# The last strips of a feed-forward block in another order: two up projections, then three down projections

## The reference, cut to what matters

```
h = rms_norm(x, pre_mlp_g)
m = jnp.square(jax.nn.relu(h @ w_up)) @ w_down        # w_up 2048 x 8192, w_down 8192 x 2048
x = x + rms_norm(m, post_mlp_g)
```

## Time and profile before

| | |
|---|---|
| timed executions | 1083.80, 1084.32, 1084.45 us, median 1084.32 |
| profiled execution | 1082.61 us, its span 1080.6 us |
| TensorE busy | 1064.9 us, 99% of the span |
| VectorE, ScalarE, GpSimd busy | 694.3, 513.4 and 94.1 us |
| granted TensorE clock, mean | 0.998 of full |

### The profile page before, as it was taken

How to read it: one execution, slowest core, us unless ns; L and a number is a source line. 1 busy time by engine, 2 the same in 40 slices (tenths; PEclk the granted TensorE clock), 3 DMA queues, 4 the chain that set the end, 5 groups by cost and what they waited for, 6 DMA issues and landing times.

```text
span 1080.6 us, 13612 instructions
## 1 busy us (share of the span) xinstructions
PE 1064.9 (99%) x4874; PEld 885.6 (82%) x4874; DVE 694.3 (64%) x766; ACT 513.4 (48%) x655; POOL 94.1 (9%) x102
## 2 busy tenths in 40 slices
PE   9999999999999999999999999999999999999996
PEld 7888888888888788888888888888888888888875
DVE  6465565558975677575665765756657656566586
ACT  6564445445544564444444444444444444444443
POOL 0010120120000420000000000000000000000003
PEclk9999999999999999999999999999999999999999
DMA  9765455453755555666656766666576665675642
GB/s 336 277 217 181 155 167 174 146 192 131 298 195 195 156 178 183 219 201 203 214 167 230 216 201 207 190 214 214 174 234 210 204 207 171 215 234 173 237 156 78
DMA packets 114655, 214.73 MB, mean 199 GB/s; under 512 B 7232, under 2 KB 20160, under 8 KB 113856
## 3 DMA queue, kind: packets, MB, share of 16 engines
q1 hardware_dynamic: 114480, 214.27, 61.0%
q10 hardware_dynamic: 144, 0.04, 0.0%
HBM read 204.84 MB, written 2.10 MB: 192 GB/s over the span
## 4 chain that ended last, share of the span: by engine, by line
PE 93%; DVE 3%; ACT 1%; issue 1%; POOL 1%; DMA 0%; SPq 0%; DVEq 0%; POOLq 0%; ACTq 0%
PE ps L635 30%; PE ps L637 30%; PE ps L636 30%; PE ps L643 2%; DVE w_lo L1182 1%; DVE aT_raw L1223 1%; DMA raw<-in_w_in 0%; PE ps L817 0%; DVE acc L1242 0%; PE ps L871 0%; PE ps L822 0%; DVE xT_lo L1408 0%; ACT u_sb L1004 0%; POOL x_res L1629 0%; ACT w_hi L917 0%
## 5 line engine op out<-in xcount | busy, mean ns | idle before, releaser
L1182 DVE TENSOR_TENSOR w_lo<-raw,w_hi 128x1024 fp32r<-128x1024 f32 (+2 forms) x383 | 470.0, 1235 | 333.9 <-ACT w_hi L917 331.4
L917 ACT ACTIVATE w_hi<-raw 128x1024 fp32r<-128x1024 f32 (+2 forms) x383 | 397.2, 1039 | 468.9 <-PE ps L637 461.3
L635 PE MATMUL ps<-w_hi,xT_hi 128*128 128x512 f32 (+1 forms) x800 | 313.1, 391 | 2.6 <-DVE xT_lo L1268 1.4
L637 PE MATMUL ps<-w_lo,xT_hi 128*128 128x512 f32 (+1 forms) x800 | 309.4, 387 | 0.0
L636 PE MATMUL ps<-w_hi,xT_lo 128*128 128x512 f32 (+1 forms) x800 | 309.2, 386 | 0.0
L635 PE MATMUL ps<-w_hi,yT_hi 128*128 128x512 f32 x672 | 263.1, 392 | 2.7 <-DVE yT_lo L1202 2.7
L637 PE MATMUL ps<-w_lo,yT_hi 128*128 128x512 f32 x672 | 261.7, 389 | 0.0
L636 PE MATMUL ps<-w_hi,yT_lo 128*128 128x512 f32 x672 | 261.6, 389 | 0.0
L635 PEld LDWEIGHTS ps<-w_hi,xT_hi 128*128 128x128 f32 x800 | 150.5, 188 | 35.0 <-issue 3.6
L637 PEld LDWEIGHTS ps<-w_lo,xT_hi 128*128 128x128 f32 x800 | 150.3, 188 | 30.5
L636 PEld LDWEIGHTS ps<-w_hi,xT_lo 128*128 128x128 f32 x800 | 150.5, 188 | 28.7
(11 more groups left out here) (147 smaller groups left out, 428.5 us busy)
## 6 DMA issues: line engine op xcount, KB each, us to landing
raw<-in_w_up SPq DMA_DIRECT2D x64, 1024.0 KB, 5.4
raw<-in_w_down SPq DMA_DIRECT2D x64, 1024.0 KB, 6.2
raw<-in_w_in SPq DMA_DIRECT2D x28, 1024.0 KB, 5.2
raw<-in_w_o SPq DMA_DIRECT2D x16, 1024.0 KB, 5.1
aT_raw<-a_blk SPq DMA_DIRECT2D x224, 32.0 KB, 1.9
raw<-in_w_uq SPq DMA_DIRECT2D x8, 576.0 KB, 4.0
raw<-in_w_ukv SPq DMA_DIRECT2D x4, 1024.0 KB, 5.0
raw<-in_w_in SPq DMA_DIRECT2D x7, 512.0 KB, 8.4
```

The costliest lines, as they stand in the source:

```text
L635: nc.tensor.matmul(dst, x_hi, hi, start=first, stop=False)
L637: mm = nc.tensor.matmul(dst, x_hi, lo, start=False, stop=last)
L917: nc.scalar.activation(w_hi[:, slot, 0:size], raw[:, raw_slot, first:first + size], ACT.Copy).then_inc(hi_ready, 1)
L1182: nc.vector.tensor_tensor(w_lo[:, slot, 0:size], raw[:, raw_slot, first:first + size], f32(w_hi[:, slot, 0:size]), ALU.subtract).then_inc( ...
```

## The change

The loop ends one iteration earlier. The tail is up strip 14, up strip 15, down strips 13, 14 and 15. Up strip 15 sums in banks 2 and 3 and no longer waits for the relu of the strip ahead. Both last strips are turned by `turn_blocks` and moved by 16 DMAs each; the transposed operands of strips 14 and 15 lie in slots 4 and 8 of `yT`. The sync engine issues the moves behind the loads of the tail's quads 2, 8 and 12.

```diff
-SHIFTED = (0, FF_STRIPS - 1)
+A_SLOT = {FF_STRIPS - 2: 4, FF_STRIPS - 1: 8}
...
-    n = len(quads) + 8 * (FF_STRIPS - 3) - 1
+    n = len(quads) + 8 * (FF_STRIPS - 4) - 1
+    for q in range(4):
+        products(up(j - 1, q, n := n + 1), tail)
+    tail.append(("relu", j - 1, n))
     for q in range(4):
         products(up(j, q, n := n + 1), tail)
+        if q == 0:
+            tail.append(("a_turn", j - 1, 0))
     tail.append(("relu", j, n))
     for q in range(4):
-        n = down(j - 1, q, n + 1)
-        for k in range(4):
-            tail.append(("mm", n, k))
-            if k == 1 and q in (1, 2):
-                tail.append(("a_shift", j, 2 * q - 1))
+        products(down(j - 2, q, n := n + 1), tail)
+        tail.append(("add", 4 * (j - 2) + q, n))
+        if q == 0:
+            tail += [("a_turn", j, 0), ("aT", j - 1, A_SLOT[j - 1])]
+    for q in range(4):
+        products(down(j - 1, q, n := n + 1), tail)
         tail.append(("add", 4 * (j - 1) + q, n))
-        if q < 2:
-            tail.append(("a_shift", j, 2 * q))
-        if q == 2:
-            tail.append(("aT", j, 4))
+        if q == 0:
+            tail.append(("aT", j, A_SLOT[j]))
...
-    LOOP = range(2, FF_STRIPS - 1)
+    LOOP = range(2, FF_STRIPS - 2)
...
-            return 6 if j == 1 else 0
+            return {1: 6, FF_STRIPS - 1: 2}.get(j, 0)
...
-                if n == NQ_TAIL + 2:
-
-                    sp.wait_ge(aT_lo_ready, FF_STRIPS - 2)
-                    move_blocks(FF_STRIPS - 1)
+                if n in (NQ_TAIL + 2, NQ_TAIL + 8, NQ_TAIL + 12):
+
+                    j = FF_STRIPS - {2: 3, 8: 2, 12: 1}[n - NQ_TAIL]
+                    sp.wait_ge(aT_lo_ready, j)
+                    move_blocks(j + 1)
...
-                        elif z["j"] > 1 and z["q"] == 0:
+                        elif 1 < z["j"] < FF_STRIPS - 1 and z["q"] == 0:
...
-                    at = 4 if z["j"] == FF_STRIPS - 1 else 0
+                    at = A_SLOT.get(z["j"], 0)
...
-                    hidden_hi(a, b, a in SHIFTED)
+                    hidden_hi(a, b, a == 0)
...
-                    turn_blocks(a, None)
+                    turn_blocks(a, (a - 1) * 256 if a > 1 else None)
```

More of the change, by code:

```diff
@@ L951, in hidden_hi @@
                 if shifted:
-                    act.wait_ge(a_turned, j + 1)
+                    act.wait_ge(a_turned, 1)
                 else:
```

## The result

| | before | changed |
|---|---|---|
| median of the timed executions (four each) | 1084.06 us | 1090.55 us (1090.02 to 1091.23) |
| profiled execution, span | 1080.6 us | 1088.7 us |
| granted clock, mean | 0.998 | 0.994 |

The ratio is 1.0063, with a 95% interval of 1.0051 to 1.0076: 6.5 us slower. 1091.5 was forecast, in a range of 1087.2 to 1095.5.

A forecast was written before the change was run, and what follows sets the result against it. PE, busy 1064.9 of 1080.6 us, was taken as the bound. Late quad 13 (8.65) minus old stall (2.9) plus clock (1.5) gave +7.2 us, from 1084.3 to 1091.5 us, range 1087.2 to 1095.5.

The forecast's parts named there:

- The two late loads: Tail loads of quads 9 and 13, each issued behind 16 moves: quad 9 starts 1.0 us late, quad 13 8.65 us.
- GpSimd's square: GpSimd's 1.9 us square in the tail, ending near 5.2 us after quad 9's landing, was claimed to delay nothing.
- L + 10.4: With L quad 9's landing at 1006.9, the end of strip 14's `yT_lo` at 1017.3, when the second moves can start.
- L + 20.8: With L quad 9's landing at 1006.9, the time quad 13's load is issued, behind the second group of moves.
- The Trainium skill's fit for a transfer: 2.0 us plus bytes by 436 GB/s: a load takes 4.4 us, the two late loads cost 3.8 us less; not used.
- The clock: PE's 7.2 us stall before quad 13 drops the clock to 1.2 GHz, costing 1.5 us, between nothing and 3.0.
- The rival with the clock unchanged: Loads late in the tail but the clock stays: +5.7 us, 1090.0 us; chance 0.16.
- What is taken out: Two large transposes replace strip 15's 16 small ones, so PE's 2.9 us wait before its down quads goes.
- The old stall: PE's wait in the tail of the kernel before, until 1049.48, for DVE's `yT_lo`: called 2.9 us.
- the loads are in time: Rival: the second moves do not delay quad 13 beyond the old stall, 1081.4 us; chance 0.06.
- Slow landings of 8.5 us: Rival: both loads behind the moves take 8.5 us, quad 13 starts 4.4 later: +11.6, 1095.9 us; chance 0.11.

The follow-up runs named there:

- fewer turns: Kernel before with 12 of strip 15's 16 small transposes and three quarters of its activations left out, so the layer is not computed: 1079.52 us.
- the add ahead: Changed kernel with VectorE's add of quad 11 put ahead of its two splits of quad 13: 1087.59 us.

## Why the prediction was right

**The two late loads: right in place, order and size.** Quad 9 was to be 1.0 us late (0.89), quad 11 1.4 in all (2.1 by the account, as quad 10 waited 0.75 where I had it at PE's pace), the second moves to start at 1017.3 (1017.68), quad 13 at 1038.8 (1038.98). The two terms of a load were each off: I took 10.0 us for 16 moves, and they took 10.96 and 11.12; I took 6.3 us to landing, and it was 5.4 and 5.3. That these errors cancel is luck. Over the six kernels with two groups in the tail, the load directly behind a group landed after 5.2 to 5.4 us in nine cases and after 6.2 or 6.3 in three, so 6.3 was one of two sizes; why stays open.

**Two terms that were wrong in the chain.** GpSimd's square was called covered. A split beside it took 0.9 us longer, which made the wait at quad 10. The end of `yT_lo` came 11.0 us after the landing in place of 10.4; quad 9 landed 0.3 us earlier than forecast, so the second moves were only 0.4 us late. And L + 10.4 and 10.05 us of moves give L + 20.45, not the L + 20.8 of the working: with it, the late quad 13 would have been 8.3 us and the forecast about 1091.1.

**The Trainium skill's fit for a transfer** (DMA: Bandwidth & Descriptors, "Anatomy of one DMA") is for another kind of queue; the estimate by it, 4.4 us, stays below these loads too (5.4 and 5.3). The trace had been the better guide.

**The clock: right that it falls, small in size.** 1.5 us were forecast from a bound of 0 to 3.0, and 2.5 were lost by the trace, 2.3 by removing it. The rival with the clock unchanged (1090.0) lies nearer to the measured 1090.55 by an accident of the next term.

**What is taken out: the mechanism right, the size not.** The term was 2.9 us, read from one profiled execution in which the clock had not fallen. The old stall cost 4.5 to 4.8 in the median (the kernels with both groups later, with both one load later, and with fewer turns): 2.9 of waiting and 1.7 of clock. I had written that this stall left the clock at 1.00, which holds for that execution only; the gap of 1.7 us between the profiled execution and the median was the sign of it, and I carried it along as a constant. With both terms at their measured size the sum is 8.9 - 4.6 + 2.5 = +6.8, against the measured +6.5. The forecast, +7.2, was so near because the old stall was taken 1.7 us too small and the clock 1.0 us too small, and the two enter with opposite signs: in part this too is luck.

**The rivals.** That the loads are in time is out for the changed kernel, and true with the moves one or two loads later. Slow landings of 8.5 us did not come for the two loads that this rival meant.

## What to carry to other kernels

A queue that carries both bulk loads and small moves has to be read as a schedule: ask of every load how long ahead of its use it is issued, and put a group of small transfers where the load behind it has the most room; here one place decided 10.9 us. When a wait on late data is found, look also at what stands behind it in each engine's program, as the add did that quad 13 needed, and at what GpSimd does beside VectorE. And before a term is read from one profiled execution, compare that execution with the spread of the times: here a stall of 2.9 us let the clock fall in some executions and not in others.

## What the runs showed of the hardware

The granted clock fell at different times after PE stopped. In the kernel before, a pause of PE of 2.9 us let it fall in one profiled execution, 3.1 us after PE stopped (clock 0.91 between 1049 and 1050), and not in the other; in the changed kernel it fell 5.2 us after PE stopped (clock 0.70 between 1037 and 1038); after the end of the matmuls before, 4.2 us. It then stayed low for 3.1 us of dense matmuls in the kernel with the first group later and for 5.7 us in the one with the add ahead. The Trainium skill (TensorE: Matmul & The Clock Gate, "HAM oscillation — how this bites in real kernels") gives a longest harmless pause that is above 2.9 us; the measured pause of 2.86 us was not harmless in one of two profiled executions and, by the mean clock, in 15 of 21 timed ones, so the measurement decides. Useless matmuls in such a pause gave back 2.3 us in one kernel and 1.7 in the other; behind the wait for the weights they cost 2.5.

A VectorE split with both operands in SBUF took 2.07 to 2.15 us in place of 1.23 when it started 0.9 us into GpSimd's square of `a_sb`, in both kernels.
